# Experts of a mixture-of-experts layer: split fp32 products over the whole array, or true fp32 over its four column quarters

## The reference, cut to what matters

```python
def swiglu(h, w_gu, w_down):
    g, u = jnp.split(h @ w_gu, 2, axis=-1)
    return (jax.nn.silu(g) * u) @ w_down

def moe_swiglu(h, router_w, w_gu, w_down):
    logits = jnp.einsum('bsd,de->bse', h, router_w, preferred_element_type=jnp.float32)
    top_v, top_i = lax.top_k(logits, EXPERT_TOPK)
    probs = jax.nn.softmax(top_v, axis=-1)
    gate = jnp.einsum('bsk,bske->bse', probs, jax.nn.one_hot(top_i, N_EXPERTS, dtype=jnp.float32))
    y = jnp.zeros_like(h)
    for e in range(N_EXPERTS):
        y = y + gate[..., e:e + 1].astype(h.dtype) * swiglu(h, w_gu[e], w_down[e])
    return y
```

## Time and profile before

| what | value |
|---|---|
| median of 3 runs | 1343.56 us (1342.73 to 1345.66) |
| span of the profiled execution | 1341.0 us; the page gives no other time of this execution |
| median over that span | 2.6 us more |
| TensorE, weight loads, VectorE, ScalarE busy | 98%, 81%, 77%, 68% |
| expert stage | 578 us to the end |
| granted TensorE clock, mean | 0.998 |

### The profile page before, as it was taken

The page is one execution under the profiler, slowest core; times in us unless marked ns, Lnnn a source line. Parts: engine busy times, 40 slices in busy tenths (PEclk is TensorE's granted clock), DMA queues, the critical chain, the costliest instruction groups (busy, mean ns, idle before and its releaser), DMA issues.

```text
span 1341.0 us, 17732 instructions
## 1 busy us (share of the span) xinstructions
PE 1320.5 (98%) x6332; PEld 1089.3 (81%) x6332; DVE 1034.0 (77%) x963; ACT 911.9 (68%) x996; POOL 87.8 (7%) x67
## 2 busy tenths in 40 slices
PE   9999999999999999999999999999999999999997
PEld 7867888888898777888888888888888888888885
DVE  5886675544467866689898898898898998988984
ACT  6688745444366877467687787686776876876873
POOL 0420000000012200000000000000010000000000
PEclk9999999999999999999999999999999999999999
DMA  8634456554466334889999999999999999999992
GB/s 289 201 95 150 154 170 217 189 188 157 147 197 214 95 127 157 302 311 396 341 377 390 377 381 391 369 382 388 370 382 385 366 389 365 382 390 368 382 391 51
DMA packets 172905, 381.22 MB, mean 284 GB/s; under 512 B 9098, under 2 KB 29236, under 8 KB 172852
## 3 DMA queue, kind: packets, MB, share of 16 engines
q1 hardware_dynamic: 169904, 370.01, 76.6%
q0 software_dynamic: 2304, 8.39, 2.4%
q10 hardware_dynamic: 644, 2.12, 0.4%
HBM read 374.20 MB, written 6.29 MB: 284 GB/s over the span
## 4 chain that ended last, share of the span: by engine, by line
PE 93%; ACT 3%; DVE 3%; issue 1%; DMA 1%; DVEq 0%; POOLq 0%; ACTq 0%
PE ps L1130 18%; PE ps L1132 18%; PE ps L1131 18%; PE ps L702 11%; PE ps L704 10%; PE ps L703 10%; PE ps L1196 1%; ACT w_hi L1314 1%; PE ps L834 1%; ACT mix L1304 1%; PE ps L827 1%; PE ps L887 1%; DVE mix L1736 1%; PE ps L1211 1%; DVE mix L1733 1%
## 5 line engine op out<-in xcount | busy, mean ns | idle before, releaser
L1965 DVE TENSOR_TENSOR w_lo<-mix,w_hi 128x2048 fp32r<-128x2048 f32 (+1 forms) x192 | 408.1, 2149 | 67.4 <-ACT w_hi L1549 65.8
L1549 ACT CAST w_hi<-mix 128x2048 fp32r<-128x2048 f32 (+1 forms) x190 | 340.7, 1810 | 85.5 <-PE ps L1132 85.5
L1698 DVE TENSOR_TENSOR w_lo<-raw,w_hi 128x2048 fp32r<-128x2048 f32 (+3 forms) x93 | 197.2, 2126 | 108.5 <-ACT w_hi L1314 107.8
L1130 PE MATMUL ps<-w_hi,eT_hi 128*128 128x512 f32 x704 | 279.0, 396 | 0.0
L1132 PE MATMUL ps<-w_hi,eT_lo 128*128 128x512 f32 x704 | 274.4, 390 | 0.0
L1131 PE MATMUL ps<-w_lo,eT_hi 128*128 128x512 f32 x704 | 274.4, 390 | 0.0
L1314 ACT CAST w_hi<-raw 128x2048 fp32r<-128x2048 f32 (+3 forms) x93 | 165.5, 1783 | 119.3 <-PE ps L704 107.2
L1965 DVE TENSOR_TENSOR w_lo<-raw,w_hi 128x2048 fp32r<-128x2048 f32 (+1 forms) x96 | 193.2, 2032 | 17.0 <-ACT w_hi L1549 16.1
L1549 ACT CAST w_hi<-raw 128x2048 fp32r<-128x2048 f32 (+1 forms) x96 | 163.4, 1713 | 48.0 <-PE ps L1132 44.4
L702 PE MATMUL ps<-w_hi,hT_hi 128*128 128x512 f32 (+1 forms) x464 | 179.7, 387 | 1.5 <-DVE w_lo L1978 0.9
L704 PE MATMUL ps<-w_hi,hT_lo 128*128 128x512 f32 (+1 forms) x464 | 176.5, 380 | 0.0
(11 more groups left out here) (207 smaller groups left out, 1487.0 us busy)
## 6 DMA issues: line engine op xcount, KB each, us to landing
mix<-in_expert_w_gate_up_dram SPq DMA_DIRECT2D x111, 1024.0 KB, 10.1
raw<-in_expert_w_gate_up_dram SPq DMA_DIRECT2D x49, 1024.0 KB, 8.5
mix<-in_expert_w_down_dram SPq DMA_DIRECT2D x48, 1024.0 KB, 11.0
raw<-in_w_in_dram SPq DMA_DIRECT2D x28, 1024.0 KB, 5.3
raw<-in_expert_w_down_dram SPq DMA_DIRECT2D x24, 1024.0 KB, 12.5
raw<-in_dense_w_gate_up_dram SPq DMA_DIRECT2D x20, 1024.0 KB, 5.1
mix<-in_expert_w_down_dram SPq DMA_DIRECT2D x25, 512.0 KB, 7.7
raw<-in_dense_w_down_dram SPq DMA_DIRECT2D x9, 1024.0 KB, 4.9
```

Of the source, the lines that this page charges most:

```text
L1130: pe.matmul(out_, l_hi, w_hi[q][:, cols], start=first, stop=False, skip_group_check=True)
L1549: act.copy(w_hi[q][:, 0:m], e_raw[raw_of(p, first)][:, 0:m]).then_inc(e_hi_ready, 1)
L1698: dve.tensor_tensor(w_lo[q][:, 0:m], raw[u % RAW][:, 0:m], w_hi[q][:, 0:m].bitcast(F32), ALU.subtract).then_inc(split, 1)
L1965: dve.tensor_tensor(w_lo[q][:, 0:m], e_raw[raw_][:, 0:m], w_hi[q][:, 0:m].bitcast(F32), ALU.subtract).then_inc(e_split, 1)
```

## The change

Each expert's item now holds up to 96 tokens (`CAP` = 96) as three groups of 32. A matmul is plain fp32 with 32 stationary columns and writes one quarter (`strip(q)`, 32 PSUM partitions); four in a row go to the four quarters with different weight columns. The weights aren't split any more: the host lays the expert weights out as 24 units per expert of 128 x 2816 (rows of 11,264 bytes), in the order of use, and SyncE loads them whole into twelve buffers (`SLOTS`), free as soon as TensorE has used them. The hidden columns come in two pieces (`PIECES`) of four times 352. VectorE turns hidden values and gathered rows in 32x32 blocks (`dve.transpose`), where TensorE did. Rows are gathered and added as three groups of 128 rows of 1 KB. Mixers, dense block and routing are as before.

The core of the diff (expert code alone; loads, waits and item loops):

```diff
-CAP = 128
+CAP = 96
 PASSES = -(-T // CAP)
-E_RAW = 9
-PER_ITEM = 6 * FF
+STRIPS = 4
+STRIP = P // STRIPS
+GROUPS = CAP // STRIP
+KT_E = D // P
+PIECES = 2
+PIECE = DFF // STRIPS // PIECES
+KT_D = PIECE // STRIP
+QUARTER = D // STRIPS
+E_UNIT = STRIPS * 2 * PIECE
+E_BLOCKS = E_UNIT // QUARTER
+DN_UNITS = KT_D * STRIPS // E_BLOCKS
+PER_ITEM = PIECES * (KT_E + DN_UNITS)
+SLOTS = 12
...
+def packed_experts(gate_up, down):
+    e = gate_up.shape[0]
+    g = gate_up.reshape(e, STRIPS, KT_E, STRIP, 2, STRIPS, PIECES, PIECE).transpose(0, 6, 2, 1, 3, 5, 4, 7)
+    d = down.reshape(e, STRIPS, PIECES, KT_D, STRIP, STRIPS, QUARTER).transpose(0, 2, 3, 5, 1, 4, 6)
...
-                        raw_free(i, p)
-                        load_dn(p, e if j else e_before, g, piece, first)
...
+            def load(i, p, e, place, first=False):
+                slot_free(i, p)
+                s_ = slot_of(p, first)
+                sp.dma_start(units[s_][:, :], a["experts"][e, place]).then_inc(unit_in[s_], 16)
...
-            def three_e(out_, left, q, cols, first, final):
-                l_hi, l_lo = left
-                pe.matmul(out_, l_hi, w_hi[q][:, cols], start=first, stop=False, skip_group_check=True)
-                pe.matmul(out_, l_hi, w_lo[q][:, cols], start=False, stop=False, skip_group_check=True)
-                return pe.matmul(out_, l_lo, w_hi[q][:, cols], start=False, stop=final, skip_group_check=True)
...
+            def gate_up_e(i, c, first):
+                for b in range(KT_E):
+                    p = gu_pos(c, b)
+                    unit_ready(i, p, first)
+                    unit = units[slot_of(p, first)]
...
+                    for g in range(GROUPS):
...
+                        for gu in range(2):
+                            for q in range(STRIPS):
+                                at = (2 * q + gu) * PIECE
+                                last = pe.matmul(ps[2 * g + gu][strip(q), 0:PIECE], eT[:, g, STRIP * b:STRIP * (b + 1)],
+                                                 unit[:, at:at + PIECE], start=b == 0, stop=b == KT_E - 1, skip_group_check=True)
...
+                    last.then_inc(e_used, 1)
+                    if c == 1 and b == 1:
...
+                            pe.wait_ge(y_out, i * GROUPS)
+                        places(i + 2)
...
+            def down_block(c, k, g, s, p0, first):
+                u, blk = divmod(STRIPS * k + s, E_BLOCKS)
+                unit = units[slot_of(p0 + u, first)]
+                at = (g % 2) * QUARTER
+                return pe.matmul(ps[6 + g // 2][strip(s), at:at + QUARTER], hidT[c][:, g, STRIP * k:STRIP * (k + 1)],
+                                 unit[:, blk * QUARTER:(blk + 1) * QUARTER], start=c + k == 0 and g % 2 == 0,
+                                 stop=c == 1 and k == KT_D - 1, skip_group_check=True)
...
             def item(i, first=False):
...
                 gate_up_e(i, 0, first)
                 if first:
                     places(1)
                 else:
-                    down_last(i)
+                    down_e(i, 1, first)
...
+                gate_up_e(i, 1, first)
+                down_e(i, 0, first)
...
+            def hidden_e(i, c):
+                for g in range(GROUPS):
+                    n = i * (2 * GROUPS) + (GROUPS * c + g + 1)
+                    dve.wait_ge(e_silu, n)
+                    dve.tensor_tensor(e_act[:, g, :], e_act[:, g, :], ps[2 * g + 1][:, 0:PIECE], ALU.mult).then_inc(hid_done, 1)
+                    dve.wait_ge(hid_done, n)
+                    dve.transpose(hidT[c][:, g, :], e_act[:, g, :]).then_inc(hidT_set, 1)
...
             def gathered(i):
+                dve.wait_ge(e_used, unit_no(i, gu_pos(1, KT_E - 1)) + 1)
+                dve.wait_ge(rows_in, i * (16 * GROUPS) + 16 * GROUPS)
+                for g in range(GROUPS):
+                    dve.transpose(eT[:, g, :], x_rows[:, g, :]).then_inc(eT_set, 1)
...
+            def add_rows(i):
+                if i:
+                    pool.wait_ge(rows_added, 16 * GROUPS * i)
+                pool.sem_inc(rows_landed, 1)
+                for g in range(GROUPS):
+                    pool.wait_ge(y_out, GROUPS * i + g + 1)
+                    pool.indirect_dma_start(out_quarters, bass.IndirectOffsetOnAxis(rows_now[:, g:g + 1], 0), y_rows[:, g, :], None,
+                                            compute_op=ALU.add).then_inc(rows_added, 16)
```

More of the change, by code:

```diff
@@ L36 @@
 NEXP, TOPK = 8, 2
-CAP = 128
+CAP = 96
 PASSES = -(-T // CAP)
+SLOT0 = tuple(min(k * CAP, T - CAP) for k in range(PASSES))
 ITEMS = NEXP * PASSES
@@ L650, in load_item, with filled_ @@
-            def load_item(i, e, e_before):
-                first = e_before is None
-                for j in range(FF):
-                    for piece in range(up_pieces(j)):
-                        p = up_at(j) + piece
-                        raw_free(i, p)
-                        load_up(i, p, e, j, piece, first)
-                    g = j - 1 if j else FF - 1
-                    if first and j == 0:
+            def filled_(*key):
+                t_ = tile[key]
+                sp.wait_ge(filled[t_.bank], t_.fill)
@@ new lines, in slot_free @@
+            def slot_free(i, p):
+                n = unit_no(i, p)
+                if not (isinstance(n, int) and n < SLOTS):
+                    sp.wait_ge(e_used, n + (1 - SLOTS))
+                elif n == 0:
+                    filled_("yT", DEPTH - 1, 1, 1)
+                elif n == 1:
+                    for t in range(NT):
+                        for b in range(2):
+                            filled_("br", DEPTH - 1, 1, t, b)
+                elif n in (2, 3):
+                    sp.wait_ge(split, NU + n - 3)
+                elif n == 4:
+                    t_ = tile["mT", DEPTH - 1, 1, 1]
+                    sp.wait_ge(drained[t_.bank], t_.done)
+                    sp.dma_start(g_row, a["ffn_norm"][DEPTH - 1].partition_broadcast(P)).then_inc(g_row_in, 16)
+                elif n == 6:
+                    sp.wait_ge(used, used_count[U["wo", DEPTH - 1, 1]])
+                elif n == 9:
+                    filled_("wo", DEPTH - 1, 1, 1)
@@ L660, in load_item @@
+            def load(i, p, e, place, first=False):
+                slot_free(i, p)
+                s_ = slot_of(p, first)
+                sp.dma_start(units[s_][:, :], a["experts"][e, place]).then_inc(unit_in[s_], 16)
+            def load_item(i, e, e_before):
+                for p in range(PER_ITEM):
+                    before = dn_pos(1) <= p < dn_pos(1) + DN_UNITS
+                    if before and e_before is None:
                         continue
[L661 to L664 removed]
+                    load(i, p, e_before if before else e, place_of(p), e_before is None)
@@ L675, in _ @@
                         load_item(e + k * NEXP, e, e - 1)
-            for piece in range(2):
-                sp.wait_ge(e_split, last * PER_ITEM + (PER_ITEM + piece - 1 - E_RAW))
-                load_dn(piece, NEXP - 1, FF - 1, piece, False)
+            for n in range(DN_UNITS):
+                load(last + 1, n, NEXP - 1, place_of(dn_pos(1) + n))
         @block.tensor
@@ L1190, in turn_e, with strip, unit_ready @@
-            def turn_e(i, j, first):
-                pe.wait_ge(hid_done, i * FF + (j + 1))
-                if not (first and j == 0):
-                    pe.wait_ge(e_turned, i * FF + j)
-                for b in range(BLOCKS[j]):
-                    last = pe.transpose(ps[2][:, b * P:(b + 1) * P], e_hid[:, b * P:(b + 1) * P], ident)
-                last.then_inc(turn_done, 1)
+            def strip(q):
+                return slice(STRIP * q, STRIP * (q + 1))
+            def unit_ready(i, p, first):
+                pe.wait_ge(unit_in[slot_of(p, first)], loads_of(i, p))
```

578 lines of the change are left out of this document (227 added, 351 removed).

## The result

The changed kernel takes **1323.58 us** (median of 4 runs, 1322.86 to 1324.07) against 1343.14 us for the kernel before beside it: 0.985 of it, 95% interval [0.984, 0.986]. It is faster, but by 1.5% where 4.2% were forecast. The time lies in the whole range of the prediction, above the 1305 us where the forecast's own part of it ends, and close to the 1320 us of the rival "the loads become the bound". The profile says that it wasn't that one.

The account below looks back on a forecast made before the run. TensorE was taken to bound the kernel, with the loads close behind. Start 577.5 + 8 items x 87.4 + end 8.0 = 1284.7 us of span, plus 2.6 for the median of runs: 1287 us, range 1264 to 1330.

Parts of the forecast that it names:

- the forecast's own part: Whole kernel: the forecast without any rival coming true, chance 0.66, reaching from 1268 to 1305 us.
- the loads become the bound: Expert items: long rows bring only 379 GB/s, so an item takes 93.4 us of DMA; 1320 us, chance 0.15.
- Covers and new waits: Expert items: VectorE's turns and GpSimd's row fetches hide behind TensorE's products; nothing exposed, 0.4 us an item added.
- uneven seams: Expert items: an allowance of 0.4 us an item, bringing 87.0 to 87.4 us.
- The sets: TensorE's expert products: four quarters run at once, 0.60 us a gate-up set, 0.44 a down set, 86.6 us an item.
- The rival of sets that don't overlap: All 162 sets of an item: each costs 0.16 us more, 113 us an item, 1492 us; chance 0.17.
- the item of 110 us: Expert items at the skill's packing rate, three column tiles at 2.38 times one: kernel 1468 us.
- The size of an item: TensorE's expert items: 87.0 us of sets and `places`, plus 0.4 for seams, 87.4 us each, eight times.
- The loads: Weights and rows of an item at 407 GB/s: 87.0 us, deciding only above 89.4 us an item.
- The start: First gather, ahead of the expert products: 2.8 us instead of 3.6, so products start at 577.5 us instead of 578.3.
- The end: After the last products: scaling, issue and landing, 8.5 us before, taken as 8.0.
- VectorE's turns: Hidden values in 32x32 blocks: 0.4 us to four times that; three groups of multiply and turn 2.7 to 6 us, hidden.

## Why the prediction was off

**The step that failed** is "Covers and new waits", with "Nothing is exposed. For uneven seams I add 0.4 us an item": 8 x 0.4 = 3.2 us for a term that measured 6 x 8.0 = 48 us. It went through buffers, semaphores and queues of every engine, and left out the one resource that the change nearly triples: the instructions in TensorE's loop. Twice the forecast counted records of matmuls, and never what a pass of the loop comes to. A seam cost 93.6 - 85.6 = 8.0 us: 4.7 to 5.1 of pause, in four of the six passes 0.4 to 1.0 of a second one, and the rest from work at half the clock. Six seams and the end make 1322.0 - 1270.9 = 51.1 us of the span. With the items written out and the end behind them, the kernel has a span of 1270.9 us, below even the forecast of 1284.7.

**The warning was in the trace of before.** TensorE's branch over the rare case's loop took 3.74 us at the end of that kernel, where the loop's own took 0.22. It cost 1.0 us at most there (a pause that the view puts down to VectorE), as the queued matmuls of 0.227 us covered the rest. A rule was there as well: the Trainium skill (Runtime: NRT & Kernel Launch, Instruction fetch mechanics) says that code comes in blocks of 16 KiB or 256 instructions, that TensorE's memory is 128 KiB or 2048 instructions, and that a taken branch whose target lies outside the current window of two such blocks must wait for a DMA. The runs agree with the blocks (packets of 16,384 bytes) and with the wait. They disagree with a window of two blocks: bodies of 768, 914 and 1392 instructions stayed whole. And a loop can't use all 2048: 1632 and 1828 instructions did not stay. Whether part of the memory is taken by code fetched ahead (a jump over 128 instructions was nearly free, one over 512 was not) no run here tells.

**The sets** were right, the main bet: four quarters run fully at once. The 96 records of two units took 7.1 us, so a set of four takes 7.1 / 12 = 0.59 us (0.60 forecast), and 33 sets of down 14.25 us, 0.43 each (0.44). That is within 0.01 us of the bare cost behind the prediction's lower bound, 2 x 0.293 and 2 x 0.213. The runs with one and two quarters show the same from the other side. The rival of sets that don't overlap, at 0.17, is refuted, and so is the item of 110 us that was worked out beside it.

**The size of an item** without its seam is 85.62 us, not 87.4. Over eight items this term was 14 us too high: 162 sets at some 0.008 us too much are 1.3 us of the 1.8, and the seams that weren't there the other 0.4. Without the error in this term the forecast would have been 1273 us, and farther from the result. These are two errors of opposite sign, and the range held the time through neither of its reasons: that it did is luck. (By its own terms the forecast's lower end is 577.5 + 8 x 84.8 + 10.6 = 1267 us, not 1268.)

**The loads** were priced at 407 GB/s and reached 420 to 426 in undisturbed stretches, the page's rows from 577 us on. So 35.39 MB take 83.7 us at 423 GB/s. The rival "the loads become the bound" had the right time for the wrong reason: with half the bytes 1315.7 us remained, and with all the bytes and no jumps TensorE never waited for a unit. The ceiling of 435 GB/s that the Trainium skill states (DMA: Bandwidth & Descriptors, Specifications) was nearer than my price from the rows.

**The start** came out at 577.04 us (577.5 forecast). **The end** was as forecast apart from the jump: in the fastest kernel 577 + 8 x 85.6 + 8.0 = 1270 us stands against 1270.9. **VectorE's turns** took 0.55 us for 352 columns and 0.42 for 256, the multiply 0.50 and SiLU 0.46, all near the lower bounds, and no wait of TensorE names them. GpSimd's fetches took 0.98 us each and not 2.42, its additions 1.58, and a fetch landed after 11.4 us: 19 us in place of the 24, hidden as forecast.

**The clock** was forecast at 1.00 and was 0.97 to 0.98 over the items: each jump's pause was followed by a stretch at half.

## What to carry to other kernels

When a change makes matmuls smaller and more numerous, count the instructions of one pass of each engine's loop, and look at the records of the branches: 0.2 us means that the body stays in the engine's memory, 6 us that its start is fetched anew; here half-clock work stood behind each such pause once the queued matmuls were short. Below some 1400 instructions a loop on TensorE was free, at 1632 it cost 8 us a pass; then write the passes out, or shorten the body, and put the rare case behind the usual one, so that no far branch stands between two matmuls. A queue of short matmuls hides little: 3.6 us of long ones stood behind a branch in the kernel before, 1.2 us of short ones in the changed one.

## What the runs showed of the hardware that was not expected

- A jump on TensorE to code that isn't held takes 5.9 to 6.8 us with the DMA engines full (6.6 to 7.6 in the loop of 1632 instructions), 4.5 to 4.9 us with them at a mean share of 0.64, and 3.3 to 3.8 us with them nearly empty (the branch at the end).
- It doesn't matter whether it goes back or forward, nor, beyond 512 instructions, how far; it matters where in its block the target lies. A target 14 instructions ahead of a block's end cost a second pause of 4 us, and moving the code by 24 instructions (48 waits) took it away, 9 us for two jumps.
- Plain fp32 matmuls of 32 columns on the four column quarters, issued in turn, overlap fully: 85.62 us an item with one, two or four quarters at work.
- Rows of 11,264 bytes reach 420 to 426 GB/s on one core; the best window before had 407.

What stays open: the exact size at which a body stops being held, between 1392 and 1632 instructions (the kernel with 1632 and the one with the branches over unused code were each measured in a single run), whether the place of the body within its blocks moves it, and why the branches of the body of 1632 took longer than those of 2640.
